# Memory keys and values on split operands, and VectorE's work between two index searches

## What is computed

```python
xn = rmsnorm(h, norm_mix_g)
q, k, v, iq, ik, iw, u, qm = split(xn @ w_in)
y_attn = dsa_attention(rope(q), rope(k), v, rope(iq), rope(ik), iw)   # index scores, top 64 keys for each query
y_pool = multiscale_pool(u, pool_w_group, pool_scale)                  # pooled, then a small mix by group
kv = rmsnorm(mem, mem_norm_g) @ w_mem_kv                               # 256 memory tokens
y_mem = softmax(qm @ km.T / 8) @ vm                                    # 4 heads
gates = sigmoid(xn @ w_gate + b_gate)
merged = gates[0] * (y_attn @ w_proj_attn) + gates[1] * (y_pool @ w_proj_pool) + gates[2] * (y_mem @ w_proj_mem)
h = h + merged @ w_out
h = h + moe(rmsnorm(h, norm_ffn_g))                                    # top 4 of 32 experts, biases b_up and b_down
out = rmsnorm(h, norm_final_g)
```

## Time and profile before

| | |
|---|---|
| median of 3 runs | 1146.21 us (1145.75 to 1147.42) |
| the profiled execution | 1147.78 us, its span 1145.9 us |
| PE busy | 1099.3 us, 96% |
| DVE busy | 310.5 us, 27% |
| ACT busy | 198.1 us, 17% |
| POOL busy | 146.1 us, 13%, all of it before 225 us |
| HBM read | 441.13 MB |

### The profile page before, as it was taken

How to read it: one execution, slowest core, us unless ns; L and a number is a source line. 1 busy time by engine, 2 the same in 40 slices (tenths; PEclk the granted TensorE clock), 3 DMA queues, 4 the chain that set the end, 5 groups by cost and what they waited for, 6 DMA issues and landing times.

```text
span 1145.9 us, 14165 instructions
## 1 busy us (share of the span) xinstructions
PE 1099.3 (96%) x5702; PEld 506.2 (44%) x5702; DVE 310.5 (27%) x692; ACT 198.1 (17%) x364; POOL 146.1 (13%) x67
## 2 busy tenths in 40 slices
PE   8999999999999999999999999999999999999996
PEld 7888999843333333333333333333333333333332
DVE  4587565332111111211111111211111111111112
ACT  5454554420100001000000010000000100000002
POOL 5862667700000000000000000000000000000000
PEclk9999999999999999999999999999999999999999
DMA  9664447999999999999999999999999999999995
GB/s 356 241 218 148 165 151 294 388 420 426 428 428 428 430 430 427 428 428 429 430 430 427 428 428 429 430 428 428 428 428 429 429 429 428 428 428 430 429 428 234
DMA packets 50100, 443.11 MB, mean 387 GB/s; under 512 B 6122, under 2 KB 9628, under 8 KB 25500
## 3 DMA queue, kind: packets, MB, share of 16 engines
q1 hardware_dynamic: 48448, 442.17, 92.3%
q10 hardware_dynamic: 1628, 0.62, 0.2%
HBM read 441.13 MB, written 1.05 MB: 386 GB/s over the span
## 4 chain that ended last, share of the span: by engine, by line
PE 63%; DMA 22%; SPq 7%; DVE 5%; ACT 2%; issue 1%; POOL 0%; DVEq 0%
PE psum L1567 25%; PE psum L1242 15%; PE psum L1602 13%; DMA ring<-in_w_up 13%; DMA my_area<-in_w_up 9%; SPq L516 7%; PE psum L1531 3%; DVE gate_area L1164 1%; DVE gate_area L1162 1%; DVE gate_area L1168 1%; PE psum L1589 1%; ACT gate_area L815 1%; PE psum L1576 1%; PE psum L1317 1%; PE psum L1339 1%
## 5 line engine op out<-in xcount | busy, mean ns | idle before, releaser
L1567 PE MATMUL psum<-ring,gate_area 128*64 128x512 f32 x1024 | 231.4, 595 | 11.3 <-DMA ring<-in_w_up 10.8
L581 POOL TENSOR_TENSOR unit_lo<-ring,unit_hi 128x1024 fp32r<-128x1024 f32 (+1 forms) x62 | 145.6, 2356 | 77.3 <-ACT unit_hi L616 77.3
L809 ACT ACTIVATE psum<-gate_area 128x512 f32<-128x512 f32 x32 | 19.2, 601 | 762.3 <-DVE gate_area L1160 762.3
L1160 DVE TENSOR_SCALAR gate_area<-psum 128x512 f32<-128x512 f32 x32 | 22.1, 692 | 457.0 <-PE psum L1576 457.0
L1567 PEld LDWEIGHTS psum<-ring,gate_area 128*64 128x64 f32 x1024 | 70.9, 137 | 160.9 <-issue 130.3
L1602 PE MATMUL psum<-ring,gate_area 128*64 128x512 f32 x512 | 116.1, 595 | 4.0 <-ACT gate_area L815 4.0
L1173 DVE COPY pT_s<-psum 128x512 f32<-128x512 f32 x32 | 22.1, 692 | 220.1 <-PE psum L1602 220.1
L616 ACT ACTIVATE unit_hi<-ring 128x1024 fp32r<-128x1024 f32 (+1 forms) x62 | 64.2, 1036 | 51.2 <-PE psum L1242 47.3
L1567 PE MATMUL psum<-my_area,gate_area 128*64 128x512 f32 x256 | 60.7, 595 | 8.3 <-DMA my_area<-in_w_up 8.3
L1531 PE MATMUL psum<-pT_s,putT 64*128 64x512 f32 x264 | 65.6, 615 | 0.8 <-DVE pT_s L1173 0.8
L1602 PEld LDWEIGHTS psum<-ring,gate_area 128*64 128x64 f32 x512 | 35.3, 136 | 68.9 <-issue 59.9
(11 more groups left out here) (238 smaller groups left out, 1148.2 us busy)
## 6 DMA issues: line engine op xcount, KB each, us to landing
ring<-in_w_up SPq DMA_DIRECT2D x64, 2048.0 KB, 40.9
ring<-in_w_down SPq DMA_DIRECT2D x32, 2048.0 KB, 40.3
qe_area<-in_w_up SPq DMA_DIRECT2D x16, 2048.0 KB, 42.4
xv_area<-in_w_up SPq DMA_DIRECT2D x16, 2048.0 KB, 43.3
pl_area<-in_w_down SPq DMA_DIRECT2D x16, 2048.0 KB, 41.8
gm_area<-in_w_up SPq DMA_DIRECT2D x16, 2048.0 KB, 41.9
my_area<-in_w_up SPq DMA_DIRECT2D x16, 2048.0 KB, 44.6
late_slot<-in_w_down SPq DMA_DIRECT2D x16, 2048.0 KB, 43.2
```

The lines of the kernel that those rows point to most:

```text
L581: nc.gpsimd.tensor_tensor(lo, src, hi.bitcast(F32), ALU.subtract).then_inc(lo_ready, 1)
L809: nc.scalar.activation(psum[:, ACT_BANK, :], glu, ACT.Sigmoid, scale=ALPHA).then_inc(sig_ready, 1)
L1160: nc.vector.tensor_scalar(glu, psum[:, 0, :], LIMIT, None, ALU.min).then_inc(glu_ready, 1)
L1567: ins = nc.tensor.matmul(psum[lo:lo + SLOTS, c, :], lhsT, w[:, at:at + 512], start=(k == 0), stop=False)
```

## The change

Two things are changed.

First, the memory's keys and values are made in three passes. ScalarE writes `memT_hi` and VectorE `memT_lo` in place of `memT`. The KV block is split in four new units, 22 and 23 (the two chunks of columns for the keys, `"cols"`) and 24 and 25 (four rows of the values' half each, `"quads"`); the gates move to units 26 to 49. `kmT` and `vm` are 48 matmuls each. The splits of units 25 to 28 stand between ScalarE's copies of `kmT` and `vm`. SyncE reuses KV's slot when its last unit is split. The place of one unit in the output projection (`OUT_PLACES`) moves with the count of units.

Second, VectorE's order changes: behind the search of block 0 it empties the mix, then runs `bias_parts`, then half of the search of block 1; the other half stands behind `normalise(1)`.

```diff
 UNITS += [("QM", "cols", c) for c in range(2)]
+UNITS += [("KV", "cols", c) for c in range(2)] + [("KV", "quads", j) for j in range(2)]
 UNITS += [(f"G{g}", "cols", c) for g in range(6) for c in range(4)]
...
-OUT_PLACES = (3, 1, 4)
-assert (O_UNIT + 1) % UNIT_SLOTS == 1
+OUT_PLACES = (3, (O_UNIT + 1) % UNIT_SLOTS, 4)
...
+    if name == "KV":
+        if j == 1:
+            return "bank_filled", FILLED["kmT" if kind == "cols" else "vm"]
+        return "unit_used", 5 * (KC // 2 - 1) + (2 if kind == "cols" else 3)
...
                     before_it = FRONT[n - RING_SLOTS]
-                    if before_it in LAST_SPLIT:
-                        sp.wait_ge(lo_ready, LAST_SPLIT[before_it])
-                    else:
-                        sp.wait_ge(bank_filled, LAST_USE[before_it])
+                    sp.wait_ge(lo_ready, LAST_SPLIT[before_it])
...
-            for u in range(11, 15):
-                split(u)
+            split(11)
+            for j in range(4):
+                t = empty(("memT", j))
+                for c in range(2):
+                    k = 2 * j + c
+                    ins = nc.scalar.activation(memT_hi[:, k, :], t[:, c * M:(c + 1) * M], ACT.Copy,
+                                               scale=gT[:, KC + k:KC + k + 1])
+                ins.then_inc(memT_hi_ready, 1)
+                if j == 1:
+                    split(12)
+            split(13)
+            split(14)
...
             copy("qmT", qmT, pair)
-            act.wait_ge(bank_filled, FILLED["vm"])
+            split(25)
             copy("kmT", kmT, pair)
+            split(26)
+            split(27)
             copy("vm", vm_s, pair)
+            split(28)
...
-                u = 22 + m + UNIT_SLOTS
+                u = G_UNIT + m + UNIT_SLOTS
...
             for j in range(4):
                 t = empty(("memT", j))
+                dve.wait_ge(memT_hi_ready, j + 1)
                 for c in range(2):
                     k = 2 * j + c
-                    ins = nc.vector.tensor_scalar(memT[:, k, :], t[:, c * M:(c + 1) * M], gT[:, KC + k:KC + k + 1],
-                                                  None, ALU.mult)
+                    ins = nc.vector.scalar_tensor_tensor(out=memT_lo[:, k, :], in0=t[:, c * M:(c + 1) * M],
+                                                         scalar=gT[:, KC + k:KC + k + 1], in1=memT_hi[:, k, :].bitcast(F32),
+                                                         op0=ALU.mult, op1=ALU.subtract)
...
             take_top(0, 0, TOPK // 8)
-            take_top(1, 0, TOPK // 8)
             t = empty("mix")
...
             bias_parts()
+            take_top(1, 0, TOPK // 16)
             for n in range(2):
                 maxima(n)
             for n in range(2):
                 normalise(n)
+            take_top(1, TOPK // 16, TOPK // 16)
...
-            n = block_arrived(pe, "KV")
             pe.wait_ge(dve_emptied, EMPTIED["memT", 3])
-            w = ring_block(n, 512)
-            done(project_T(fill("kmT"), w, 0, memT, 2))
+            t = fill("kmT")
+            for c in range(2):
+                chunk_T(t[:, c * M:(c + 1) * M], c == 1, (memT_hi, memT_lo))
             t = fill("vm")
-            for b in range(B):
+            units = [next_unit()]
+            for b in range(B):
+                s = slice(b * P, (b + 1) * P)
                 for k in range(KC):
-                    ins = nc.tensor.matmul(t[:, b * 256:(b + 1) * 256], memT[:, k, b * P:(b + 1) * P], w[:, k, 256:512],
-                                           start=(k == 0), stop=(k == KC - 1))
+                    if b == 0 and k == 4:
+                        units.append(next_unit())
+                    hi, lo = units[k // 4]
+                    ins = three_passes(t[:, b * 256:(b + 1) * 256], (memT_hi[:, k, s], memT_lo[:, k, s]),
+                                       (hi[:, k % 4, :], lo[:, k % 4, :]), k == 0, k == KC - 1)
+                    if b == 1 and k == 3:
+                        ins.then_inc(unit_used, 1)
             done(ins)
```

More of the change, by code:

```diff
@@ L97 @@
 UNITS += [(f"O{hf}", "rows", j) for hf in range(2) for j in range(KC // 2)]
+G_UNIT = UNITS.index(("G0", "cols", 0))
 P_UNIT = UNITS.index(("P", "cols", 0))
@@ L154 @@
         EMPTIED["br", _f, _n] = _f + 1
-LAST_USE = {"KV": FILLED["vm"]}
 LAST_SPLIT = {name: n + 1 for n, (name, _, _) in enumerate(UNITS)}
@@ L168, in unit_read @@
         if j < KC // 2 - 1:
-            return "unit_used", 5 * (KC // 2 - 1) + 1 + hf * (KC // 2 - 1) + j + 1
+            return "unit_used", 5 * (KC // 2 - 1) + 3 + hf * (KC // 2 - 1) + j + 1
         return "bank_filled", FILLED["out", B - 1, hf]
@@ L204, in unit_at @@
                     for part, o in (("hi", hi_at), ("lo", lo_at))]
[L206 to L209, removed]
+        ahead = [n for n in range(UNIT_SLOTS) if n != OUT_PLACES[1]]
+        starts = {ahead[0]: 0, ahead[1]: 8, OUT_PLACES[1]: 16, 3: 24}
+        unit_buf = [unit_at(n, down_at + starts[n] * UNIT_W, down_at + (starts[n] + 4) * UNIT_W) for n in range(4)]
         xT_lo = nc.alloc_sbuf_tensor_at("xT_lo", [P, KC, S], F32R, offset=down_at + 24 * UNIT_W)
@@ L229, in hybrid_layer_kernel @@
         qk_area = at("qk_area", [P, 2 * HEADS // 2 * S], qe_at)
+        memT_lo = at("memT_lo", [P, KC, M], qe_at + 2 * PIECE_W, F32R)
         xT_at = nc.sbuf_base + (-nc.sbuf_base) % 32
@@ L237, in hybrid_layer_kernel @@
         memT = at("memT", [P, KC, M], memT_at)
+        memT_hi = at("memT_hi", [P, KC, M], memT_at, F32R)
         memT_parts = at("memT_parts", [P, 8, S], memT_at, F32R)
@@ L374, in hybrid_layer_kernel @@
         xT_hi_ready = sem("xT_hi_ready")
+        memT_hi_ready = sem("memT_hi_ready")
         got_eps = sem("got_eps")
@@ L435, in unit_views @@
             w = ring_block(FRONT.index("PA" if name == "P" else name), cols)
-            src = w[:, 2 * j:2 * j + 2, :] if kind == "rows" else w[:, :, j * P:(j + 1) * P]
+            if kind == "quads":
+                src = w[:, 4 * j:4 * j + 4, 256:512]
+            else:
+                src = w[:, 2 * j:2 * j + 2, :] if kind == "rows" else w[:, :, j * P:(j + 1) * P]
             k, n = src.shape[1], src.shape[2]
@@ L1311, in _, with chunk_T @@
             done(ins)
[L1313 to L1321, removed]
+            def chunk_T(t, last_of_job, rhs=(xT_hi, xT_lo)):
                 hi, lo = next_unit()
                 for k in range(KC):
-                    ins = three_passes(t, (hi[:, k, :], lo[:, k, :]), (xT_hi[:, k, :], xT_lo[:, k, :]), k == 0,
+                    ins = three_passes(t, (hi[:, k, :], lo[:, k, :]), (rhs[0][:, k, :], rhs[1][:, k, :]), k == 0,
                                        k == KC - 1)
```

## The result

The changed kernel takes 1150.85 us (median of 6 runs, 1149.89 to 1151.67), the kernel before 1146.51 us in the same comparison: a ratio of 1.0037, 95% interval 1.0026 to 1.0047, or 4.3 us slower. The profiled execution of the changed kernel took 1151.01 us with a span of 1148.8 us.

The account below looks back on a forecast made before the run. TensorE's chain in the front part was taken to bound the kernel, by starting the expert weight stream. With TensorE's 1.94 us gain swallowed, stalls of +2.0 and +1.3 summed to +3.3 us: 1149.5 us, range 1144.3 to 1151.2.

Parts of the forecast that it names:

- two stalls: TensorE waits at the second set of pT transposes, +2.0 us net, and before gate 5, +1.3 us.
- the forecast's own case: VectorE's casts, copies and TENSOR_TENSORs wait for GpSimd's splits: 1149.5 us, range 1148.5 to 1150.7, chance 0.45.
- rival (c): TENSOR_TENSOR at 85.64 us meets unit 25's split: maxima(0) at 103.7 us, +4.6 us, 1150.8 us; chance 0.13.
- the first stall: TensorE's second set of pT transposes waits for VectorE's softmaxes: +2.0 us against before, swallowing the 1.94 us gained.
- What bounds the kernel: Expert part's weight stream sets its length; TensorE's chain in front starts it, so front changes move the end equally.
- TensorE's part, -1.94 us: Keys and values: two groups of 6.91 us plain fp32 replaced by two of 5.94 us on split operands, -1.94 us.
- the estimate of 3.46 us: Keys and values: three passes for four would save a quarter of 13.82 us; the sum used 1.94 instead.
- Splitting the memory's transposes, 0: ScalarE's eight activations and VectorE's second half fit in idle time: cost 0, at most about 1.5 us without that cover.
- The holds of VectorE: bias_parts under four GpSimd splits: held instructions end it at 98.5 us, not 90.8; maxima(0) at 102.4, +3.1 us.
- Rival (a): In bias_parts casts and copy don't wait for GpSimd, only TENSOR_TENSORs do: -1.9 us, 1144.4 us; chance 0.20.
- (b): The cast at old line 968 slips in ahead of unit 28's split: +1.2 us, 1147.4 us; chance 0.14.
- The second half of the search, +1.3 us: Behind normalise(1), maxima(2) starts 3.0 us late, 1.75 us is regained; TensorE waits before gate 5, +1.3 us.

Follow-up runs that it names:

- late biases: Changed kernel with the search of block 1 whole ahead of the softmaxes and bias_parts behind take_o(0): 1144.44 us, 0.9986 of the kernel before.
- Order only: Kernel before with only VectorE's new order (search of block 1 halved, bias_parts between the searches), keys and values as before: 1146.63 us, ratio 1.0001.
- 16 dummies: Changed kernel with 16 dummy matmuls on TensorE ahead of its wait for the first softmax: 1150.66 us, 1.0034 of the kernel before.
- passes only: Changed kernel with VectorE's old order (whole search of block 1, then mix, then bias_parts): 1150.81 us, 1.0035 of the kernel before.
- casts moved: Changed kernel with the last three small instructions of bias_parts moved behind take_o(1): 1147.63 us, 1.0009 of the kernel before.

## Why the prediction was right, and where it was not

Forecast was 1149.5 us, +3.3 us by two stalls worth +2.0 and +1.3; measured is 1150.85, +4.3 us. That is just outside the 1148.5 to 1150.7 of the forecast's own case. It lies inside the whole range, 1144.3 to 1151.2, whose upper end was drawn for rival (c), and (c) did not happen: here the range held by luck. The direction and the first stall were not luck. By its steps:

- **What bounds the kernel.** Right. The expert part didn't change, and the end moved with the first expert piece (4.50 and 4.34 us). In the version with late biases it moved the other way, -2.22 and -2.3 us.
- **TensorE's part, -1.94 us.** Right in kind, a little small: 2 x (5.76 - 6.91) = -2.3 us, and without stalls the way is 2.22 us shorter. TensorE therefore reached its stand some 0.4 us earlier than forecast, which changes nothing in the time of the changed kernel, since VectorE ends that stand. True fp32 is four passes by the Trainium skill, page FP8 and Floating Point Precision, section TensorE Precision Notes; the estimate of 3.46 us made from it, three passes at three quarters of the time, is not borne out: 11.52 us of 13.82 is 0.83.
- **Splitting the memory's transposes, 0.** Right: in the changed kernel ScalarE still idles 0.20 us ahead of the splits of units 12 and 13, and TensorE waits for none of them.
- **The holds of VectorE.** Right one by one (lines of the changed kernel, 988 is the prediction's 968): copy, cast at 985, cast at 987 and cast at 988, each behind one split; the first softmax at 102.21 (forecast 102.4), the second set of transposes at 105.80 + 0.81 = 106.61 against 104.65, **+1.96** (forecast +2.0). Rival (a), casts pass freely, is out, and so is (b), the cast at 988 slips in. Copies and casts are among the instructions that can take the ports shared with GpSimd by the Trainium skill, page SBUF — State Buffer, section Who interferes with whom. The changed kernel's trace agrees for casts (2.64 and 2.61 us against 0.55), which the trace before couldn't show. Rival (c), a mask instruction caught by unit 25's split, missed by little: it ended at 84.92 and the split is listed from 84.87. Order only shows that the new order alone costs nothing, late biases that the passes cost nothing where VectorE's held instructions are covered. With the old order the passes do cost (+4.1 us by the medians), by another stall that the prediction didn't look for.
- **The second half of the search, +1.3 us.** The mechanism was there, but not in the sum. The first softmax of the next pair starts 5.75 us behind the last `normalise(1)` instruction (105.03 + 0.62, then 111.40), where 5.7 was forecast. Unit 31 was ready at 116.12 + 2.39 = 118.51 us (119.32 on the old scale; the forecast makes it 119.4), but TensorE came only at 116.80 + 2.97 = 119.77. The step that failed is the last one, in which TensorE runs on at its usual prices behind the first stall: the fall of the clock stood at nothing in the sum. Behind a stand of 3.56 us its clock was at the lower level for some 6 us, and the transposes, scores and two gates took 0.65 + 0.95 + 0.95 = **2.55 us** more than in the earlier trace rows. In the place of +1.3 stands +2.55, which hides the 1.3: 1.96 + 2.55 = 4.5 us. With the clock held up the stall appears with 1.21 us. That the total came within about 1 us of the forecast is so in part because the unforeseen cost hid a forecast one.

What stays open is the price of the clock in the medians: the traces give it 0.9 us (the way of changed less that of 16 dummies) to 1.3 us (2.55 - 1.21) net of the stall that it hides, but the medians of changed and 16 dummies can't be told apart. The price of the second half of the search without the first stall rests on the traces as well: 1.0 us of way, while the intervals of the two versions (0.9977 to 0.9995 and 0.9985 to 1.0003) overlap.

## What to carry to other kernels

Before work of one engine is moved, look at which engine's new instructions it will meet there, not only at whether its own engine has time. In these traces the form decides on VectorE: MAX8 and MATCH_REPLACE8 (0.43 and 0.41 us) and the mix read from PSUM (0.88 for two) ran at their usual price under GpSimd's splits, while casts, copies, tensor_scalar and two-source instructions from SBUF waited for the end of the split that was running, up to 2.2 us each (2.41 against 0.22 for the cast of 128 elements). So a few tiny ones in a row can cost more than all their work. And a stall of TensorE of a few us is to be priced with what runs behind it at half clock.

## What was not expected of the hardware

After a stand of 3.56 us, in a stretch of the front part where TensorE is otherwise solidly busy, the granted clock was at 0.50 for about 6 us, in both traces of the changed kernel. The clock fell in passes only too, with a stand of 3.86 us; in casts moved, with a stand of 1.08 us, it did not. In the expert part of both kernels the clock reads 1.00 in spite of many gaps (0.25 us each up to 741 us, and waits for weights of up to 1.2 us behind it). And where VectorE and GpSimd take turns, the delay goes both ways: with the late biases two TENSOR_TENSORs of 0.96 us took 3.05 us, and two splits of 2.4 us each took 5.49 us together.
